# A hybrid decoder block on one core: the value projection of the recurrent layer in three float32r passes instead of native float32 products

## The chip, the cores and the metric

One core of a Trainium2 chip runs the whole program; the other cores are idle. The metric is the device time of one execution in microseconds (us), as the median of several runs. Before the change it is 1592.16 us (three runs, 1592.12 to 1593.12). Engines are named as the profile names them: PE is TensorE, DVE is VectorE, ACT is ScalarE, POOL is GpSimd, SP is SyncE, which issues the weight loads.

## What is computed

Two decoder layers over 272 tokens (16 meta tokens and 256 of the sequence), width 1024: sliding-window attention and a dense SwiGLU, then RWKV-7 time mixing and top-2-of-8 routed SwiGLU experts. The change sits in the time mixing of the second layer. Cut to what matters:

```python
xx = jnp.pad(h, ((0, 0), (1, 0), (0, 0)))[:, :-1] - h
xr, xw, xk, xv, xa, xg = [h + xx * mix[i] for i in range(N_MIX)]
r = xr @ w_r
k = xk @ w_k
v = xv @ w_v                       # 272 x 1024 by 1024 x 1024, float32
w = -jax.nn.softplus(-(w0 + jnp.tanh(xw @ w1) @ w2)) - 0.5
a = jax.nn.sigmoid(a0 + (xa @ a1) @ a2)
g = jax.nn.sigmoid(xg @ g1) @ g2
...
decay = jnp.exp(-jnp.exp(to_h(w)))
...                                # the recurrence over tokens, 16 heads of 64
return (y * g) @ w_o
```

## The kernel before

**Layout.** Activations of the recurrent layer lie with their 1024 channels as 8 chunks (KC) of 128 partitions, and the 272 tokens along the free dimension. A projection makes 8 output blocks of 128 channels (two heads each, a "pair"); a block is 8 matmuls of 128x128 weights against 128x272 activations, summed in one PSUM bank. `project(j)` does one block: j = 0 to 7 are keys, 8 to 15 receptance (r), 16 to 23 values. It takes PSUM bank j % 4, so it waits until ACT has copied out block j - 4 (`pr_ev`). The products are native float32: each matmul of the program shows as two records of the profile.

**The other form of product.** Elsewhere (attention, dense FFN, experts) the kernel forms float32 products from float32r passes. Operands are split into a high part (ACT: a copy to float32r, `ffn_high`) and a low part (DVE: the operand minus its high part, `ffn_low`); `split3` (lines 811 to 814) issues high x high, high x low and low x high.

**The order around the values.** Everything here is written out by hand, per engine, in program order; semaphores tie the engines.

- PE: key blocks; the small projections of decay, gates and step size (lines 1100 to 1127); then blocks 8 to 23 by `project`. After each of blocks 12 to 19 it does one `per_head` product (line 1087), which sums r times k over each head of a pair for the bonus term; it waits for that product's operand from DVE (`rk_ok`). After block 23 come the products of the recurrence (from line 1164 on).
- ACT, in its loop over j = 8 to 23: `take(j)` copies block j out of PSUM (line 1831); for j = 10 to 17 `decays(j - 10)`, three exponentials (lines 1866 to 1868), which wait for DVE's cumulative sums of that pair (`cum_ok`); for j = 13 to 20 it copies a bonus product out (line 1877).
- DVE: mixes the inputs (`mixes`, line 2352), among them the value input (`mixes(0, 3, ...)`), which goes to `xm[0]`; three long passes over keys and step sizes (lines 2394 to 2399); then a loop over the 8 pairs, in each of which: line 2405 makes the operand of `per_head` (`rk_ok`), line 2407 the scan, line 2410 the difference (`cum_ok`), then it waits for ACT's exponentials (`dec_exp`), and lines 2412 to 2416 scale five arrays.
- SP: weights of 2 MB in slots of SBUF. Slots 0 and 1 hold w_k, then w_r, then w_o; slots 2 and 3 hold the small matrices, then w_v. The two halves of w_o are loaded when blocks 8 to 11 and 12 to 15 are done (`pr_mm` 12 and 16). The queue then waits for the end of the recurrence (`ot_mm`, from line 1328 on PE) and starts the stream of the expert weights, which runs to the end of the program.

The lines that load the weights and that order the DVE loop:

```python
for s, w, n, s_, used in (..., (2, rwkv_w_v, 0, mix_used, 2),
                          (3, rwkv_w_v, 1, l2_mm, 24), (0, rwkv_w_o, 0, pr_mm, 12), (1, rwkv_w_o, 1, pr_mm, 16)):
    sp.wait_ge(s_, used)
    load(s, slot_k[s], cols(w[0], n))
```

Of the kernel before, what the change touches and what calls it, by code (L numbers as in the profile page):

```python
# [24 lines left out]
P = 128  # L25
# [45 lines left out]
def build(nc, x, meta_tokens, mixer_norm, ffn_norm, attn_w_qkv, attn_q_norm, attn_k_norm, attn_sinks, attn_w_o,  # L71
# [4 lines left out]
    with ctx:  # L76
        def sb(name, shape, dt=F32):
            return ctx.enter_context(nc.sbuf_tensor(name, shape, dt))
# [108 lines left out]
        with nc.sbuf_tensor("under_pT", [P, KC * T + 6 * HALF], F32), nc.sbuf_tensor("pT_hi", [P, 2, 8, P], F32R) as pT_hi, \  # L187
                nc.sbuf_tensor("pT_lo", [P, 2, 8, P], F32R) as pT_lo:
            pass
        arena = sb("arena", [P, ARENA])  # L190

        def area(off, *dims):
# [112 lines left out]
        ht_mm, ht_cp, yt_mm, yn_ok, gn_act, gn_ss, y_ok, wo2_mm, acc_ok = [sem(n) for n in (  # L305
            "ht_mm", "ht_cp", "yt_mm", "yn_ok", "gn_act", "gn_ss", "y_ok", "wo2_mm", "acc_ok")]
# [3 lines left out]
        sel_ok, xg_mm, xg_act, xg_dve, st_mm, st_ev, utok_hi_ok, utok_lo_ok, dn_mm, ye_hi_ok = [sem(n) for n in (  # L310
            "sel_ok", "xg_mm", "xg_act", "xg_dve", "st_mm", "st_ev", "utok_hi_ok", "utok_lo_ok", "dn_mm", "ye_hi_ok")]
# [3 lines left out]
        out_sem, utT_dve, own_mm = sem("out_sem"), sem("utT_dve"), sem("own_mm")  # L315
# [142 lines left out]
        def _(sp):  # L458
# [66 lines left out]
            for s, w, n, s_, used in ((0, rwkv_w_r, 0, pr_mm, 4), (1, rwkv_w_r, 1, pr_mm, 8), (2, rwkv_w_v, 0, mix_used, 2),  # L525
                                      (3, rwkv_w_v, 1, l2_mm, 24), (0, rwkv_w_o, 0, pr_mm, 12), (1, rwkv_w_o, 1, pr_mm, 16)):
                sp.wait_ge(s_, used)
                load(s, slot_k[s], cols(w[0], n))
# [214 lines left out]
        def _(pe):  # L743
# [309 lines left out]
            def project(j):  # L1053
                which, m = j // KC, j % KC
                cols_ = slice(META if which == 1 else 0, T)
                s = (0, 0, 2)[which] + m // 4
                if m == 0 and which:
                    pe.wait_ge(mix_ok, 3 + which)
                if m % 4 == 0:
                    pe.wait_ge(slot_in[s], 16 * {0: 1, 1: 1, 2: 4, 3: 5}[s] + (16 if which == 1 else 0))  # L1060
                if j >= 4:
                    pe.wait_ge(pr_ev, j - 3)
                for k in range(KC):
                    last = mm(ps[:, j % 4, cols_], slot_k[s][:, k, (m % 4) * P:(m % 4 + 1) * P], xm[(0, 1, 0)[which]][:, k, cols_],  # L1064
                              start=(k == 0), stop=(k == KC - 1))
                last.then_inc(pr_mm, 1)
# [323 lines left out]
            def tokens_turned(t, half):  # L1390
                pe.wait_ge(acc_ok, 2 * t + half + 1)
                if t == 0:
                    pe.wait_ge(yn_ok, 2)
                for q in range(4):
                    k = 4 * half + q
                    last = tr(ps[:, (6, 4)[t] + half, q * P:(q + 1) * P], acc[:, t, k * P:(k + 1) * P], ident[:, :])
                last.then_inc(utT_mm, 1)

            def logits(t, half):
                pe.wait_ge(*((utT_cp, 2 * t + half + 1) if 2 * t + half < 3 else (utT_dve, 1)))  # L1400
# [37 lines left out]
            with pe.Fori(0, n) as pas:  # L1438
# [25 lines left out]
                def turn(e):  # L1464
                    for t in range(2):
                        last = tr(ps[:, 5, t * P:(t + 1) * P], sel[:, t, e % 2, :].bitcast(F32), ident[:, :])
                    last.then_inc(st_mm, 1)
# [149 lines left out]
        def _(act):  # L1617
# [337 lines left out]
            def square_tokens(t):  # L1955
                act.wait_ge(acc_ok, 2 * t + 2)
# [147 lines left out]
        def _(dve):  # L2104
# [246 lines left out]
            def mix(k, buf, i, c0=0):  # L2351
                return v.scalar_tensor_tensor(xm[buf][:, k, c0:T], xx[:, k, c0:T], par[:, k, R_MIX + i:R_MIX + i + 1],
# [48 lines left out]

            dve.wait_ge(pads_zero, 3)
            for m in range(PAIRS):
# [6 lines left out]
                own.done(v.tensor_tensor(w_a[:, m, :], cum[:, m % 2, :], w_a[:, m, :], ALU.subtract), cum_ok)  # L2410
                dve.wait_ge(dec_exp, m + 1)
# [135 lines left out]
            def added(n):  # L2547
# [3 lines left out]
                own.done(v.tensor_tensor(acc[:, t, cs], htok[:, t, cs], ps[:, n, :], ALU.add), acc_ok)  # L2551
# [30 lines left out]
            own.done(v.tensor_copy(utT[:, 4:8, P:2 * P], ps[:, 5, :].rearrange("p (a b) -> p a b", a=4)), utT_dve)  # L2582
# [84 lines left out]
            with dve.Fori(0, n) as pas:  # L2667
# [15 lines left out]
                def gate_rows(e):  # L2683
                    dve.wait_ge(st_mm, pas + 1)
                    v.tensor_copy(selT[:, e % 2, :, :], ps[:, 5, 0:256].rearrange("p (a b) -> p a b", a=2)).then_inc(st_ev, 1)

                def collect(e, o, bank):
                    dve.wait_ge(es_mm, pas * 4 + (o + 1))
# [126 lines left out]
```

## Time and profile before

| | |
|---|---|
| runs | 1592.12, 1593.12, 1592.16 us (median 1592.16) |
| profiled execution | 1595.8 us, its span (first to last instruction) 1594.0 us |
| mean granted TensorE clock | 0.991 of full speed |
| PE busy | 1549.3 us, 97% of the span |
| DVE / ACT / POOL busy | 1219.7 / 1000.0 / 139.8 us |
| HBM read | 431.92 MB, 274 GB/s over the span |

The profiled execution is one execution of its own and 3.6 us above the median of the runs. Times in the trace count from the first instruction. In the trace the recurrent layer lies between about 397 and 655 us: the projections until 520 us, the recurrence until 609 us, then the output projection and the routing. The experts fill the rest. A matmul record lasts longer than the spacing between two records, since they are pipelined; a stretch of matmuls is therefore read from start to start.

### The profile page before, as it was taken

How to read it: one execution, taken by the hardware profiler on the slowest of the kernel's cores; microseconds unless marked ns; L12 is line 12 of the kernel's file. 1: busy time of each engine (PE TensorE's matmuls, PEld its weight loads, DVE VectorE, ACT ScalarE, POOL GpSimd, SP SyncE). 2: the span in 40 equal slices, each digit the busy share in tenths (PEclk: the TensorE clock that was granted, in tenths of full speed). 3: DMA queues.
4: the chain of work that ended last, by engine and by line, in shares of the span. 5: the costliest groups of instructions: out<-in, count | busy, mean ns of one | idle time of the engine just before them, and what ended most of it. 6: DMA issues, size and time to landing. Idle time of an engine off the chain costs nothing.

```text
span 1594.0 us, 26420 instructions
## 1 busy us (share of the span) xinstructions
PE 1549.3 (97%) x10509; PEld 1307.1 (82%) x10509; DVE 1219.7 (77%) x1165; ACT 1000.0 (63%) x1030; POOL 139.8 (9%) x195
## 2 busy tenths in 40 slices
PE   9999999999999989999999999999999999999998
PEld 7889999999778875788888888766788666788877
DVE  5565655633695574789888888999888989888898
ACT  5665344432243452577777777888777888767776
POOL 3464000000100640000000000000000000000200
PEclk9899999999999999899999999999999999999999
DMA  8105555544332006299999999999999999999996
GB/s 295 54 16 197 183 164 183 177 142 154 112 140 77 4 4 251 104 369 372 378 389 344 365 392 376 387 395 392 397 392 395 395 394 394 395 394 393 395 394 246
DMA packets 193199, 438.37 MB, mean 275 GB/s; under 512 B 10227, under 2 KB 11251, under 8 KB 193076
## 3 DMA queue, kind: packets, MB, share of 16 engines
q1 hardware_dynamic: 191452, 430.82, 73.5%
q0 software_dynamic: 1584, 5.77, 0.9%
q8 instruction: 85, 1.39, 0.4%
q14 instruction: 38, 0.31, 0.1%
q10 hardware_dynamic: 40, 0.08, 0.0%
HBM read 431.92 MB, written 4.72 MB: 274 GB/s over the span
## 4 chain that ended last, share of the span: by engine, by line
PE 79%; DVE 9%; DMA 5%; ACT 3%; issue 3%; DVEq 0%; ACTq 0%; SPq 0%; POOL 0%; POOLq 0%
PE ps L1503 13%; PE ps L1505 13%; PE ps L1504 13%; PE ps L812 7%; PE ps L814 6%; PE ps L813 6%; DVE wsplit L2673 5%; PE ps L1064 4%; DMA raw_w<-in_moe_w_up 3%; DMA raw_w<-in_moe_w_gate 3%; PE ps L1385 2%; ACT wsplit L1998 2%; PE ps L750 1%; PE ps L1541 1%; PE ps L1074 1%
## 5 line engine op out<-in xcount | busy, mean ns | idle before, releaser
L2673 DVE TENSOR_TENSOR wsplit<-raw_w,wsplit 128x2048 fp32r<-128x2048 f32 x336 | 754.4, 2286 | 68.6 <-ACT wsplit L1998 67.5
L1998 ACT ACTIVATE wsplit<-raw_w 128x2048 fp32r<-128x2048 f32 x336 | 629.9, 1920 | 78.7 <-DMA raw_w<-in_moe_w_up 31.2
L1503 PE MATMUL ps<-wsplit,xsplit 128*128 128x512 f32 x672 | 266.3, 396 | 3.4 <-DVE wsplit L2673 3.4
L1505 PE MATMUL ps<-wsplit,xsplit 128*128 128x512 f32 x672 | 262.1, 390 | 0.0
L1504 PE MATMUL ps<-wsplit,xsplit 128*128 128x512 f32 x672 | 261.7, 389 | 0.0
L1503 PEld LDWEIGHTS ps<-wsplit,xsplit 128*128 128x128 f32 x672 | 126.2, 188 | 30.8 <-DVE wsplit L2673 6.2
L1505 PEld LDWEIGHTS ps<-wsplit,xsplit 128*128 128x128 f32 x672 | 126.1, 188 | 27.2
L1504 PEld LDWEIGHTS ps<-wsplit,xsplit 128*128 128x128 f32 x672 | 126.4, 188 | 24.8
L2300 DVE TENSOR_TENSOR ffn_lo<-ffn_raw,ffn_hi 128x2048 fp32r<-128x2048 f32 x42 | 95.0, 2292 | 54.9 <-ACT ffn_hi L1787 54.7
L1503 PE MATMUL ps<-wsplit,hsplit 128*128 128x512 f32 x336 | 131.2, 390 | 2.2 <-DVE wsplit L2673 2.2
L1504 PE MATMUL ps<-wsplit,hsplit 128*128 128x512 f32 x336 | 130.8, 389 | 0.0
L1505 PE MATMUL ps<-wsplit,hsplit 128*128 128x512 f32 x336 | 130.8, 389 | 0.0
L814 PE MATMUL ps<-u_hi,ffn_lo 128*128 128x272 f32 x448 | 129.0, 288 | 0.0
L812 PE MATMUL ps<-u_hi,ffn_hi 128*128 128x272 f32 x448 | 128.9, 288 | 0.0
L813 PE MATMUL ps<-u_lo,ffn_hi 128*128 128x272 f32 x448 | 128.9, 288 | 0.0
L2048 ACT ACTIVATE arena<-ps 128x512 f32<-128x512 f32 x56 | 33.4, 596 | 110.5 <-PE ps L1505 110.5
L1530 PE MATMUL ps<-wsplit,xsplit 128*128 128x512 f32 x224 | 92.6, 414 | 10.3 <-DVE wsplit L2673 9.3
L1787 ACT ACTIVATE ffn_hi<-ffn_raw 128x2048 fp32r<-128x2048 f32 x42 | 78.6, 1904 | 37.8 <-PE ps L814 37.8
L1531 PE MATMUL ps<-wsplit,xsplit 128*128 128x512 f32 x224 | 87.8, 392 | 0.0
L812 PEld LDWEIGHTS ps<-u_hi,ffn_hi 128*128 128x128 f32 x448 | 84.6, 189 | 0.1
L813 PEld LDWEIGHTS ps<-u_lo,ffn_hi 128*128 128x128 f32 x448 | 84.2, 188 | 0.1
L814 PEld LDWEIGHTS ps<-u_hi,ffn_lo 128*128 128x128 f32 x448 | 84.1, 188 | 0.0
(476 smaller groups left out, 2547.7 us busy)
## 6 DMA issues: line engine op xcount, KB each, us to landing
raw_w<-in_moe_w_gate SPq DMA_DIRECT2D x114, 1024.0 KB, 10.6
raw_w<-in_moe_w_up SPq DMA_DIRECT2D x112, 1024.0 KB, 11.3
raw_w<-in_moe_w_down SPq DMA_DIRECT2D x112, 1024.0 KB, 10.5
ffn_raw<-in_ffn_w_up SPq DMA_DIRECT2D x14, 1024.0 KB, 5.2
ffn_raw<-in_ffn_w_gate SPq DMA_DIRECT2D x14, 1024.0 KB, 5.2
ffn_raw<-in_ffn_w_down SPq DMA_DIRECT2D x14, 1024.0 KB, 5.0
ffn_raw<-in_attn_w_qkv SPq DMA_DIRECT2D x6, 1024.0 KB, 10.7
ffn_raw<-in_attn_w_o SPq DMA_DIRECT2D x4, 1024.0 KB, 11.6
```

The lines of the kernel that those rows point to most:

```text
L812: mm(o, w_hi_, x_hi_, start=first, stop=False)
L813: mm(o, w_hi_, x_lo_, start=False, stop=False)
L814: return mm(o, w_lo_, x_hi_, start=False, stop=last_)
L1503: mm(o, x_[0], w_[0], start=first_, stop=False)
L1504: mm(o, x_[0], w_[1], start=False, stop=False)
L1505: return mm(o, x_[1], w_[0], start=False, stop=last_)
L1530: mm(o, both_parts(x_, k), whi[:, kk, :], start=(k == 0), stop=False)
L1531: last = mm(o, both_parts(x_, k), wlo[:, kk, :], start=False, stop=(k == KC - 1))
L1787: A(ffn_hi[:, m % NFH, :], ffn_raw[:, ffn_at(m), :], ACT.Copy).then_inc(hi_ok, 1)
L1998: A(wsplit[:, m % NRING, 0, :], raw_w[:, m % NRAW, :], ACT.Copy).then_inc(w_hi, 1)
L2300: v.tensor_tensor(ffn_lo[:, ffn_at(m), :], ffn_raw[:, ffn_at(m), :], ffn_hi[:, m % NFH, :].bitcast(F32), ALU.subtract).then_inc(lo_ok, 1)
L2673: v.tensor_tensor(wsplit[:, m % NRING, 1, :], raw_w[:, m % NRAW, :], wsplit[:, m % NRING, 0, :].bitcast(F32), ALU.subtract).then_inc(w_lo, 1)
```

## The change

The eight value blocks no longer use native float32 products. ACT makes the high part of the value input (one copy of 128x2176, `value_high(-1)`) and of the weights of each pair (eight copies of 128x1024), DVE the low parts (`value_low`), and PE calls `split3` 8 times per block. The low parts overwrite their sources in place; the high parts of the weights lie partly in slots 0 and 1, so w_o is loaded after block 23 (`pr_mm` 24). Three semaphores are merged to make room for two new ones (`v_part_hi`, `v_part_lo`). Cut to its core:

```diff
+        with nc.sbuf_tensor("under_vhi2", [P, KC * T], F32), nc.sbuf_tensor("vw_hi2", [P, 6, KC, P], F32R) as vw_hi2, \
...
+                nc.sbuf_tensor("xv_hi", [P, KC, T], F32R) as xv_hi:
+            pass
...
+        vw_raw = [raw_w[:, 2 * h:2 * h + 2, :].rearrange("p a (b n) -> p (a b) n", n=BLK) for h in range(2)]
+        vw_hi = [vw_hi0[:, m] for m in range(2)] + [vw_hi2[:, m] for m in range(6)]
...
-                                      (3, rwkv_w_v, 1, l2_mm, 24), (0, rwkv_w_o, 0, pr_mm, 12), (1, rwkv_w_o, 1, pr_mm, 16)):
+                                      (3, rwkv_w_v, 1, l2_mm, 24), (0, rwkv_w_o, 0, pr_mm, 24), (1, rwkv_w_o, 1, pr_mm, 24)):
...
                 if j >= 4:
                     pe.wait_ge(pr_ev, j - 3)
-                for k in range(KC):
+                if which == 2:
+                    pe.wait_ge(v_part_hi, m + 2)
+                    pe.wait_ge(v_part_lo, m + 2)
+                for k in range(KC) if which == 2 else ():
+                    last = split3(ps[:, j % 4, 0:T], vw_hi[m][:, k, :], vw_lo[:, m // 4, k, (m % 4) * P:(m % 4 + 1) * P],
+                                  xv_hi[:, k, :], xv_lo[:, k, :], k == 0, k == KC - 1)
+                for k in range(KC) if which < 2 else ():
...
+            def value_high(m):
+                if m < 0:
+                    act.wait_ge(mix_ok, 5)
+                    A(xv_hi[:, :, :], xv_raw[:, :, :], ACT.Copy).then_inc(v_part_hi, 1)
+                    return
+                act.wait_ge(slot_in[2 + m // 4], 16 * (4 + m // 4))
+                if m >= 2:
+                    act.wait_ge(pr_mm, KC + (4 if m < 6 else 8))
+                A(vw_hi[m], vw_raw[m // 4][:, :, (m % 4) * P:(m % 4 + 1) * P], ACT.Copy).then_inc(v_part_hi, 1)
+
             act.wait_ge(kk_done, 1)
             for j in range(KC, 3 * KC):
                 take(j)
+                if j == KC:
+                    value_high(-1)
+                elif j == KC + 1:
+                    value_high(0)
+                    value_high(1)
+                elif KC + 3 <= j <= 2 * KC:
+                    value_high(j - KC - 1)
                 if 10 <= j < 18:
                     decays(j - 10)
...
+            def value_low(m):
+                dve.wait_ge(v_part_hi, m + 2)
+                if m < 0:
+                    v.tensor_tensor(xv_lo[:, :, :], xv_raw[:, :, :], xv_hi[:, :, :].bitcast(F32), ALU.subtract).then_inc(v_part_lo, 1)
+                    return
+                cs = slice((m % 4) * P, (m % 4 + 1) * P)
+                v.tensor_tensor(vw_lo[:, m // 4, :, cs], vw_raw[m // 4][:, :, cs], vw_hi[m].bitcast(F32),
+                                ALU.subtract).then_inc(v_part_lo, 1)
+
+            value_low(-1)
             dve.wait_ge(pads_zero, 3)
             for m in range(PAIRS):
                 dve.wait_ge(pr_ev, KC + 1 + m)
...
                 own.done(v.tensor_tensor(w_a[:, m, :], cum[:, m % 2, :], w_a[:, m, :], ALU.subtract), cum_ok)
+                value_low(m)
                 dve.wait_ge(dec_exp, m + 1)
```

How the instructions stand on three engines. On DVE, from the last long pass over all keys to the second pair of the loop; the line numbers of the changed kernel are 10 to 43 higher. Before:

```order
L2399 TENSOR_TENSOR arena<-arena 128x8x272
L2405 SCALAR_TENSOR_TENSOR arena<-arena,par 128x256
L2407 SCALAR_TENSOR_TENSOR arena<-reset,arena 128x320
L2410 TENSOR_TENSOR arena<-arena 128x320
L2412 TENSOR_TENSOR arena<-arena 128x256
L2413 COPY chunkdecay<-arena 128x5
L2414 TENSOR_TENSOR arena<-arena 128x320
L2415 TENSOR_TENSOR arena<-arena 128x320
L2416 SCALAR_TENSOR_TENSOR arena<-arena 128x320
L2405 SCALAR_TENSOR_TENSOR arena<-arena,par 128x256
```

and now:

```order
L2432 TENSOR_TENSOR arena<-arena 128x8x272
L2438 TENSOR_TENSOR xv_lo<-xv_raw,xv_hi 128x2176
L2448 SCALAR_TENSOR_TENSOR arena<-arena,par 128x256
L2450 SCALAR_TENSOR_TENSOR arena<-reset,arena 128x320
L2453 TENSOR_TENSOR arena<-arena 128x320
L2441 TENSOR_TENSOR vw_lo<-raw_w,vw_hi0 128x8x128
L2456 TENSOR_TENSOR arena<-arena 128x256
L2457 COPY chunkdecay<-arena 128x5
L2458 TENSOR_TENSOR arena<-arena 128x320
L2459 TENSOR_TENSOR arena<-arena 128x320
L2460 SCALAR_TENSOR_TENSOR arena<-arena 128x320
L2448 SCALAR_TENSOR_TENSOR arena<-arena,par 128x256
```

The low part of the value input (L2438) stands ahead of the whole loop, and the low part of one pair's weights (L2441) in each of its eight rounds, between the difference and the first of the scaled arrays.

On ACT, from the last copies of the gate blocks to the second set of exponentials, before:

```order
L1859 ACTIVATE arena<-ps 128x256 x2
L1831 ACTIVATE arena<-ps 128x256 x3
L1866 ACT_TABLE_LOAD
L1866 ACTIVATE arena<-arena 128x320
L1867 ACTIVATE arena<-arena 128x320
L1868 ACTIVATE arena<-arena 128x320
L1831 ACTIVATE arena<-ps 128x256
L1866 ACTIVATE arena<-arena 128x320
```

and now:

```order
L1875 ACTIVATE arena<-ps 128x256 x2
L1847 ACTIVATE arena<-ps 128x256
L1889 ACTIVATE xv_hi<-xv_raw 128x2176
L1847 ACTIVATE arena<-ps 128x256
L1894 ACTIVATE vw_hi<-raw_w 128x1024 x2
L1847 ACTIVATE arena<-ps 128x256
L1882 ACT_TABLE_LOAD
L1882 ACTIVATE arena<-arena 128x320
L1883 ACTIVATE arena<-arena 128x320
L1884 ACTIVATE arena<-arena 128x320
L1847 ACTIVATE arena<-ps 128x256
L1894 ACTIVATE vw_hi<-raw_w 128x1024
```

The high parts stand behind the copies out of PSUM, six of them one per round ahead of the exponentials.

On SP the order is the same and the waits differ only in their counts:

```order
L473 DMA raw_w<-in_rwkv_w_v 128x8x512 [waits mix_used]
L473 DMA raw_w<-in_rwkv_w_v 128x8x512 [waits l2_mm]
L473 DMA arena<-in_rwkv_w_o 128x8x512 [waits pr_mm] x2
L565 DMA arena<-in_ffn_norm 128x1024 [waits ot_mm]
L562 DMA raw_w<-in_moe_w_gate 128x4x512 [waits w_lo] x2
```

Nothing stands between the two loads of w_o and the wait for the end of the recurrence, so a later load of w_o holds back no other load that is due before that wait ends.

## Rows read from the trace of the kernel before

**Rows 1.** The page: busy time of PE; the chain that ended last, by line

```profile
PE 1549.3 (97%) x10509; PEld 1307.1 (82%) x10509; DVE 1219.7 (77%) x1165; ACT 1000.0 (63%) x1030; POOL 139.8 (9%) x195
...
PE ps L1503 13%; PE ps L1505 13%; PE ps L1504 13%; PE ps L812 7%; PE ps L814 6%; PE ps L813 6%; DVE wsplit L2673 5%; PE ps L1064 4%; DMA raw_w<-in_moe_w_up 3%; DMA raw_w<-in_moe_w_gate 3%; PE ps L1385 2%; ACT wsplit L1998 2%; PE ps L750 1%; PE ps L1541 1%; PE ps L1074 1%
```

**Rows 2.** Stretches (blocks 16-19, 20-23, recurrence): PE PEld DVE ACT POOL, clock, DMA

```profile
488.79:505.18 16.39, 16.39 (x73) 13.68 (x72) 11.29 (x27) 6.38 (x19) 0.00 (x0) 1.00 0.36 129
505.18:520.00 14.82, 14.82 (x65) 11.97 (x63) 4.41 (x12) 2.88 (x10) 0.00 (x0) 1.00 0.00 0
520.00:549.00 29.00, 28.47 (x933) 25.92 (x934) 15.15 (x25) 13.14 (x23) 16.66 (x16) 1.00 0.02 5
```

**Rows 3.** Timeline of PE: start us, us, line, shape, count [idle before]

```profile
488.79 3.83 PE L1064 MATMUL ps<-arena 128*128 128x272 f32 x16
492.46 0.59 PE L1087 MATMUL ps<-arena,headones 128*128 128x256 f32 x2
...
504.75 0.59 PE L1087 MATMUL ps<-arena,headones 128*128 128x256 f32 x2
505.18 14.83 PE L1064 MATMUL ps<-arena 128*128 128x272 f32 x64
520.55 1.16 PE L1166 MATMUL ps<-arena 64*64 64x64 f32 x64 [0.53 <-issue]
```

**Rows 4.** Float32r matmuls of line 812: ns min/median/max, first and last start

```profile
L812 PE MATMUL ps<-u_hi,ffn_hi x448: 284/287/492, 139.2 to 308.6; 128*128 128x272 f32 x150
```

**Rows 5.** Timeline of DVE, the last long passes and the loop over pairs

```profile
467.50 2.42 DVE L2399 TENSOR_TENSOR arena<-arena 128x2176 f32<-128x2176 f32 x1
469.95 0.48 DVE L2405 SCALAR_TENSOR_TENSOR arena<-arena,par 128x256 f32<-128x256 f32 x1
...
471.20 0.49 DVE L2410 TENSOR_TENSOR arena<-arena 128x320 f32<-128x320 f32 x1
472.95 0.43 DVE L2412 TENSOR_TENSOR arena<-arena 128x256 f32<-128x256 f32 x1 [1.25 <-ACT arena L1868]
...
474.57 0.48 DVE L2405 SCALAR_TENSOR_TENSOR arena<-arena,par 128x256 f32<-128x256 f32 x1
...
502.24 0.48 DVE L2405 SCALAR_TENSOR_TENSOR arena<-arena,par 128x256 f32<-128x256 f32 x1
```

**Rows 6.** Timeline of ACT: blocks 8 and 9 taken, last exponential of pairs 0 and 7

```profile
463.15 0.38 ACT L1831 ACTIVATE arena<-ps 128x256 f32<-128x256 f32 x1 [3.13 <-PE ps L1064]
466.55 0.38 ACT L1831 ACTIVATE arena<-ps 128x256 f32<-128x256 f32 x1 [3.01 <-PE ps L1064]
...
472.46 0.45 ACT L1868 ACTIVATE arena<-arena 128x320 f32<-128x320 f32 x1
...
504.75 0.45 ACT L1868 ACTIVATE arena<-arena 128x320 f32<-128x320 f32 x1
```

**Rows 7.** Groups by form, 280 to 300 us: splits of 128x1088 in the FFN

```profile
L2335 DVE TENSOR_TENSOR hid_lo<-hid,hid_hi 128x1088 fp32r<-128x1088 f32 x1 | 1.3, 1293 | 1.2 <-ACT hid_hi L1812 1.2
...
L1812 ACT ACTIVATE hid_hi<-hid 128x1088 fp32r<-128x1088 f32 x1 | 1.1, 1112 | 8.0 <-DVE hid L2333 8.0
```

**Rows 8.** Timeline of SP: issue of w_v, of w_o, and the end of its wait

```profile
446.44 13.55 SPq L463 DMA_DIRECT2D arena<-in_rwkv_w_v  x2
473.44 15.48 SPq L463 DMA_DIRECT2D arena<-in_rwkv_w_o  x2
...
609.49 0.35 SPq L555 DMA_DIRECT2D arena<-in_ffn_norm  x1
```

**Rows 9.** The page's DMA issues: KB each, median us from issue to landing

```profile
arena<-in_rwkv_w_o SPq DMA_DIRECT2D x2, 2048.0 KB, 8.2
```

**Rows 10.** Timeline of PE: the first matmuls that read w_o

```profile
609.38 7.13 PE L1385 MATMUL ps<-arena 128*128 128x512 f32 x16
```

**Rows 11.** The chain that ended last, a piece among the experts

```profile
1100.24 13.71 DMA raw_w<-in_moe_w_gate
```

**Rows 12.** Groups by form, 655 to 1590 us: the experts' low parts

```profile
L2673 DVE TENSOR_TENSOR wsplit<-raw_w,wsplit 128x2048 fp32r<-128x2048 f32 x335 | 752.1, 2286 | 68.6 <-ACT wsplit L1998 67.5
```

More of the change, by code:

```diff
@@ L189, in build @@
             pass
+        with nc.sbuf_tensor("under_vhi2", [P, KC * T], F32), nc.sbuf_tensor("vw_hi2", [P, 6, KC, P], F32R) as vw_hi2, \
+                nc.sbuf_tensor("under_vlo", [P, 2 * KC * P], F32), nc.sbuf_tensor("vw_lo", [P, 2, KC, BLK], F32R) as vw_lo, \
+                nc.sbuf_tensor("vw_hi0", [P, 2, KC, P], F32R) as vw_hi0, nc.sbuf_tensor("under_xv", [P, KC * T - 2 * KC * P], F32), \
+                nc.sbuf_tensor("xv_lo", [P, KC, T], F32R) as xv_lo, nc.sbuf_tensor("under_xvhi", [P, 2 * KC * BLK - 2 * KC * T], F32), \
+                nc.sbuf_tensor("xv_hi", [P, KC, T], F32R) as xv_hi:
+            pass
+        with nc.sbuf_tensor("under_xvraw", [P, 2 * KC * T + 4 * KC * BLK], F32), nc.sbuf_tensor("xv_raw", [P, KC, T], F32) as xv_raw:
+            pass
+        vw_raw = [raw_w[:, 2 * h:2 * h + 2, :].rearrange("p a (b n) -> p (a b) n", n=BLK) for h in range(2)]
+        vw_hi = [vw_hi0[:, m] for m in range(2)] + [vw_hi2[:, m] for m in range(6)]
         arena = sb("arena", [P, ARENA])
@@ L304, in build @@
             "rhs_mm", "rhs_ev", "u_mm", "u_ev", "ot_mm", "gb_ok", "s_mm", "s_ok", "rank_next")]
[L305 to L306 removed]
+        ht_mm, ht_cp, yt_mm, yn_ok, gn_act, gn_ss, y_ok, wo2_mm, acc_utT_ok = [sem(n) for n in (
+            "ht_mm", "ht_cp", "yt_mm", "yn_ok", "gn_act", "gn_ss", "y_ok", "wo2_mm", "acc_utT_ok")]
         n4_std_exp, utok_ok, utT_mm, utT_cp, choice_mm, choice_ok = [sem(n) for n in (
@@ L525, in _ @@
             for s, w, n, s_, used in ((0, rwkv_w_r, 0, pr_mm, 4), (1, rwkv_w_r, 1, pr_mm, 8), (2, rwkv_w_v, 0, mix_used, 2),
-                                      (3, rwkv_w_v, 1, l2_mm, 24), (0, rwkv_w_o, 0, pr_mm, 12), (1, rwkv_w_o, 1, pr_mm, 16)):
+                                      (3, rwkv_w_v, 1, l2_mm, 24), (0, rwkv_w_o, 0, pr_mm, 24), (1, rwkv_w_o, 1, pr_mm, 24)):
                 sp.wait_ge(s_, used)
-                load(s, slot_k[s], cols(w[0], n))
+                load(s, vw_raw[n] if w is rwkv_w_v else slot_k[s], cols(w[0], n))
             we_g = moe_w_gate[0].rearrange("e (k p) n -> e p k n", p=P)
@@ L1390, in tokens_turned @@
             def tokens_turned(t, half):
-                pe.wait_ge(acc_ok, 2 * t + half + 1)
+                pe.wait_ge(acc_utT_ok, 2 * t + half + 1)
                 if t == 0:
@@ L1399, in logits @@
             def logits(t, half):
-                pe.wait_ge(*((utT_cp, 2 * t + half + 1) if 2 * t + half < 3 else (utT_dve, 1)))
+                pe.wait_ge(*((utT_cp, 2 * t + half + 1) if 2 * t + half < 3 else (acc_utT_ok, 5)))
                 for k in range(4 * half, 4 * half + 4):
@@ L1466, in turn @@
                         last = tr(ps[:, 5, t * P:(t + 1) * P], sel[:, t, e % 2, :].bitcast(F32), ident[:, :])
-                    last.then_inc(st_mm, 1)
+                    last.then_inc(es_mm, 1)
                 def scatter(e, o, bank):
@@ L2351, in mix @@
             def mix(k, buf, i, c0=0):
-                return v.scalar_tensor_tensor(xm[buf][:, k, c0:T], xx[:, k, c0:T], par[:, k, R_MIX + i:R_MIX + i + 1],
+                return v.scalar_tensor_tensor((xm[buf] if i != 3 else xv_raw)[:, k, c0:T], xx[:, k, c0:T], par[:, k, R_MIX + i:R_MIX + i + 1],
                                               uT[:, k, 1 + c0:T + 1], ALU.mult, ALU.add)
@@ L2550, in added @@
                 cs = slice(h * BLK, (h + 1) * BLK)
-                own.done(v.tensor_tensor(acc[:, t, cs], htok[:, t, cs], ps[:, n, :], ALU.add), acc_ok)
+                own.done(v.tensor_tensor(acc[:, t, cs], htok[:, t, cs], ps[:, n, :], ALU.add), acc_utT_ok)
             def root(t):
@@ L2581, in _ @@
             dve.wait_ge(utT_mm, 4)
-            own.done(v.tensor_copy(utT[:, 4:8, P:2 * P], ps[:, 5, :].rearrange("p (a b) -> p a b", a=4)), utT_dve)
+            own.done(v.tensor_copy(utT[:, 4:8, P:2 * P], ps[:, 5, :].rearrange("p (a b) -> p a b", a=4)), acc_utT_ok)
             root(1)
```

12 lines of the change are left out of this document (6 added, 6 removed).

## Prediction

> **What bounds the kernel now.** I read the page first. PE is busy for 97% of the span, and nearly all of the chain that ended last is PE's or the experts' splits; line 1064, the native projections, has 4% of it [rows 1]. So a microsecond taken off those projections can be worth a microsecond, if PE really is what waits for nothing there. The stretches say so for both halves of the value blocks: PE is busy without a gap from 488.79 to 520.00 us, at a granted clock of 1.00, which is the 2.4 GHz level [rows 2]. The PE timeline gives the unit: block 16 starts at 488.79 and the per-head product behind it at 492.46, so a block takes 3.67 us. From a per-head product to the next block it is 0.43 us (504.75 to 505.18). Blocks 20 to 23 run back to back from 505.18 for 14.83 us, to 520.01, and the recurrence starts at 520.55 [rows 3].
>
> The second thing to read is DVE. Its loop over pairs starts at 469.95; the next round starts at 474.57 and the eighth at 502.24, so seven rounds take 32.29 us, 4.61 each [rows 5]. Each round begins with the operand (0.48 us) of the per-head product that PE does behind block 12 + m. The eighth operand is ready at 502.24 + 0.48 = 502.72, and PE wants it at 504.75 [rows 3, 5]: 2.03 us of slack today. That slack is what the change runs into.
>
> **PE alone.** Removed: 64 native products, 8 blocks of 3.67 us. Added: 192 float32r matmuls of 128x272. The dense FFN has the same shape and the same `split3`: in its first part 1344 such matmuls (448 on each of three lines) start between 139.2 and 308.6 us, that is 169.4 / 1343 = 0.126 us each [rows 4]. So a block becomes 24 x 0.126 = 3.03 us and saves 0.64 us; all eight save 5.1 us. That is the most PE can get by this row. A native block spread over four passes per product is 3.67 / 32 = 0.115 us per pass, so the two rows price a pass differently; I take the FFN's, because it is the very instruction, shape and clock.
>
> The Trainium skill counts in passes ("FP8 and Floating Point Precision", TensorE Precision Notes: true FP32 takes four passes through the array). By that rule three passes would be 3/4 of 3.67, or 2.75 us a block. The FFN's spacing disagrees with it by a tenth.
>
> **DVE ahead of the loop.** New is the low part of the value input, 128x2176. It stands behind the pass of line 2399, which is of the same size and takes 2.42 us, and the following instruction started 2.45 us after it (467.50 to 469.95), with a settling wait in it. I take 2.35 us for the shift of the whole loop; 2.2 to 2.5 would do. Its high part is ready in time: ACT is free between blocks 8 and 9, 463.53 to 466.55 [rows 6], and a copy of 128x2176 is twice the 128x1088 copy of 1.11 us [rows 7], so it ends near 465.8, before 469.95.
>
> **DVE in the loop.** New in each round is a low part of 128x1024. Between the row of 128x1088 (1.293 us) [rows 7] and those of 128x320 (0.49) [rows 5] it comes to 1.23 us. In a round the difference ends at 471.69 (1.74 us in), and DVE then idles 1.25 us until ACT's third exponential ends at 472.91 [rows 5, 6]. The low part goes exactly there: 471.69 + 1.23 = 472.92. I cost it at nothing; its cover is this wait, and if the cover fails the price is up to 1.23 us a round. It needs its high part: those of pairs 0 and 1 follow block 9 on ACT (466.9, some 1.05 us each by the 1.11 of rows 7, so done by 469.1, before block 10 and before the exponentials), the others are made one round ahead of the pair. w_v's second half is issued near 460.0 and lands about 8.2 us later [rows 8, 9], well before its first reader behind block 13. ACT's work in a round grows by 1.05 us to about 3 us of 4.61. Nothing.
>
> **PE with DVE's gate.** The operands now come at 469.95 + 2.35 + 4.61 m + 0.48: 491.2 (m = 4), 495.8, 500.4 and 505.1 (m = 7). PE needs them behind blocks 16 to 19. Block 16 starts at 488.79 as before (the r blocks before it are not touched, and their gates keep a slack of over 1 us), ends at 491.8, no wait. Block 17 starts at 492.25, ends at 495.3 and waits 0.5. Block 18 then runs from 496.4 to 499.4 and waits 1.0; block 19 from 501.0 to 504.0 and waits 1.1. With 0.1 us for the signal and 0.43 behind the per-head product, block 20 starts at 505.60 instead of 505.18: **0.42 us later**, in spite of four faster blocks. Blocks 20 to 23 have no per-head product behind them; their low parts are ready (the last, pair 7's, at about 507.6) and they gain 4 x 0.64 = 2.56 us. PE reaches the recurrence 2.56 - 0.42 = **2.1 us** earlier. What else the recurrence needs: the DVE loop ends near 509.3 instead of 506.9, still ahead of 517.9.
>
> **SP.** w_o's two loads go from 473 and 489 us to about 518. At 8.2 us each [rows 9] they land by 535; they are first read at 609.38 [rows 10]. Nothing. They now run under the recurrence, where DMA was idle (share 0.02) and PE issues most densely, 933 matmuls in 29 us [rows 2]. No row shows that stretch with a transfer in it, so: between 0 and, if instruction supply suffered, the 0.5 us of one "issue" gap [rows 3] a few times. I take 0. The merged semaphores cost nothing: waits stay where they were.
>
> **Does it survive the experts?** The expert stream is issued when the recurrence ends on PE (609.49) [rows 8], so transfers, PE and splits all move by the same 2.1 us. Sum against the profiled execution: 1595.8 - 2.1 = 1593.7. That execution is 3.6 us above the median of the runs; against the median, 1592.16 - 2.14 = **1590.0 us**.
>
> **The rivals.**
> *The gate does not hold* (say, the operands keep their slack because DVE catches up): PE gains the whole 5.1 us, 1587.0. Against it: a DVE round has no idle time left but what the low part takes. 5%.
> *A float32r pass costs what a native pass costs*, 0.115 us: a block saves 0.92, and 4 x 0.92 - 0.42 = 3.3 us, 1588.9. For it: the native block's own rate. Against it: 1344 matmuls at 0.126 us. The Trainium skill's pass count, cited above, is this case. 7%.
> *The experts swallow it*: they have their own balance of transfers and splits, such as a wait of 13.7 us for a gate tile [rows 11], and if some fixed point there decides, the time stays at 1592.2. Against it: the stream has no start of its own. 12%.
> *DVE's loop becomes the bound, and the kernel gets slower.* Place: the low part in each round. If it does not fit into the 1.25 us, because it starts only when its high part comes or because the strided read takes longer, each round grows by d and block 20 by 7 d. Fully exposed, d = 1.23: block 20 starts 8.6 us later, the sum is 2.1 - 8.6, and the time 1598.7. It turns slower from d = 0.31. For it: the fit is exact on paper, with nothing to spare. Against it: a contiguous split of twice the size runs at 2.286 us in the experts [rows 12], no sign of a slow form, and the start of an instruction overlaps the end of the one before. 8%, counting the milder cases that still end 3 us up.
> The forecast has the remaining 68%. Its own range is a gain of 1 to 3.2 us: d between -0.05 and 0.1, the shift 2.2 to 2.5, waits of PE on two more semaphores per block at up to 0.1.
>
> **The numbers.** 1590.0 us. A measurement of this kernel can tell about 0.2%, 3.2 us, from no change. Faster by more than that are the gate that does not hold (5%), most of the pass-cost case (6%, since 3.3 is just over) and the forecast's upper tail (8%): 19%. Slower by more is the DVE case, 8%. The rest, 73%, is within 0.2%, though most of it on the faster side. The range of 8 in 10 runs from 1588.0, which takes in the pass-cost case, to 1593.0, which takes in the swallowed gain and a little scatter.
>
> **What would show it.** Right: blocks of the value projection at 3.03 us from start to start; PE idle before the per-head products behind blocks 17 to 19, released by line 2448 on DVE; DVE rounds of 4.61 us from 472.3 on with hardly any idle time; block 20 at about 505.6; the recurrence at about 518.4 instead of 520.55; the first expert load at about 607.4; and from there the same length to the end. Wrong: blocks at 2.75 us; no idle time on PE before line 1103; DVE rounds over 4.9 us; a recurrence that is longer than its 89 us while w_o lands; or an expert stage that is longer by what was won.

## The result, and the profile after

The changed kernel is slower, by a little: 1595.76 us (median of 20 runs, 1593.22 to 1598.1) against 1593.25 us for the kernel before in 20 runs (1591.33 to 1596.17); the ratio is 1.0015, with a 95% interval of 1.0009 to 1.0021. By the ratio that is 2.4 us more, and the forecast was 2.1 us less. The median of the kernel before rose by 1.1 us with the further runs (1592.16 in the first three), but even with the range moved up by that, to 1594.1 us, the time lies outside it, and on the other side of no change.

The two profiled executions must not be compared by their spans. The one of the changed kernel is 2.5 us shorter (1591.5 against 1594.0). But they part long before the change. At 64.9 us, when the attention stage begins, they are within 0.1 us of each other; at its output projection, 107 us before and 102.6 us after, they are 4.3 us apart. In between, the granted clock of the one before was 0.50, the 1.2 GHz level, from about 68 to 82 us, and that of the one after was not. Two rows, busy time from 70 to 100 us, before and after; the clock, a mean over the stretch, is the third column from the right:

```profile
70.00:100.00 30.00, 29.97 (x189) 24.47 (x190) 22.83 (x86) 20.08 (x70) 12.56 (x16) 0.80 0.08 28
```

```profile
70.00:100.00 30.00, 28.66 (x217) 23.53 (x218) 26.09 (x97) 22.87 (x80) 15.44 (x20) 1.00 0.08 30
```

So I count from the start of block 8, the first block of the loop that the change touches: at 459.44 us before, at 455.08 us after. First the PE timeline of the kernel before at that place, then of the changed kernel:

```profile
459.44 17.43 PE L1064 MATMUL ps<-arena 128*128 128x256 f32 x80
```

```profile
455.08 17.43 PE L1080 MATMUL ps<-arena 128*128 128x256 f32 x80
...
491.56 0.70 PE L1103 MATMUL ps<-arena,headones 128*128 128x256 f32 x2 [0.49 <-DVE arena L2448]
...
496.17 0.70 PE L1103 MATMUL ps<-arena,headones 128*128 128x256 f32 x2 [0.90 <-DVE arena L2448]
...
500.79 0.70 PE L1103 MATMUL ps<-arena,headones 128*128 128x256 f32 x2 [0.90 <-DVE arena L2448]
...
514.12 1.16 PE L1182 MATMUL ps<-arena 64*64 64x64 f32 x64 [0.53 <-issue]
...
517.89 0.44 PE L1180 MATMUL ps<-arena 64*64 64x128 f32 x7
519.96 1.85 PE L1180 MATMUL ps<-arena 64*64 64x128 f32 x57 [1.62 <-issue]
...
524.41 0.44 PE L1192 MATMUL ps<-arena 64*64 64x64 f32 x6
526.18 0.86 PE L1192 MATMUL ps<-arena 64*64 64x64 f32 x23 [1.33 <-issue]
...
607.77 7.13 PE L1401 MATMUL ps<-arena 128*128 128x512 f32 x16
```

These rows answer to [rows 3] and [rows 10]. Three stretches come out of them:

| us | before | after | difference |
|---|---|---|---|
| block 8 to the recurrence | 61.11 | 59.04 | -2.07 |
| recurrence, to the first matmul that reads w_o | 88.83 | 93.65 | +4.82 |
| from there to the end | 984.62 | 983.73 | -0.89 |

The first line is the forecast's gain. The second takes more than twice that away. Its two rows of 1.62 and 1.33 us with "issue" are PE sitting still between two matmuls of one line. In [rows 3] the first matmul of the recurrence has an "issue" row too, with 0.53 us, and so it has here; the two others are new at that place.

The recurrence falls into two parts. The first, from its first matmul to the first of line 1239 (1255 in the changed kernel), is the one in which w_o now lands; I call it the dense part. Before, then after:

```profile
547.53 4.77 PE L1239 MATMUL ps<-arena 64*64 64x64 f32 x158
```

```profile
544.94 4.78 PE L1255 MATMUL ps<-arena 64*64 64x64 f32 x158
```

It takes 26.98 us before and 30.82 after: 3.84 of the 4.82 us. The remaining 0.98 us lies in the rest, 61.85 us before and 62.83 after, where no w_o is in flight any more. There the kernel before has small "issue" rows of its own, with no load beside them:

```profile
590.91 0.33 PE L1319 MATMUL ps<-arena 64*64 64x64 f32 x4 [0.24 <-issue]
...
595.38 0.27 PE L1328 MATMUL ps<-arena 64*64 64x64 f32 x2 [0.77 <-issue]
```

The changed kernel has 0.70 and 0.54 us in the same place.

The third line of the table is scatter: over the ten profiles of this study, all with the same code from there on, it lies between 982.9 and 985.2 us.

What runs at that moment is the load of w_o. The timeline of SP, which answers to [rows 8], and time to landing, which answers to [rows 9]:

```profile
513.62 0.99 SPq L473 DMA_DIRECT2D arena<-in_rwkv_w_o  x2
...
607.88 0.35 SPq L565 DMA_DIRECT2D arena<-in_ffn_norm  x1
```

```profile
arena<-in_rwkv_w_o SPq DMA_DIRECT2D x2, 2048.0 KB, 11.4
```

Both halves are issued half a microsecond before the recurrence starts, and they fill the DMA engines until about 527 us.

The splits are where they were planned. DVE in the changed kernel, answering to [rows 5]: the start of the loop, one round, and the start of the last round.

```profile
465.60 2.42 DVE L2438 TENSOR_TENSOR xv_lo<-xv_raw,xv_hi 128x2176 fp32r<-128x2176 f32 x1
467.94 0.48 DVE L2448 SCALAR_TENSOR_TENSOR arena<-arena,par 128x256 f32<-128x256 f32 x1
...
469.19 0.49 DVE L2453 TENSOR_TENSOR arena<-arena 128x320 f32<-128x320 f32 x1
469.59 1.22 DVE L2441 TENSOR_TENSOR vw_lo<-raw_w,vw_hi 128x1024 fp32r<-128x1024 f32 x1
470.93 0.43 DVE L2456 TENSOR_TENSOR arena<-arena 128x256 f32<-128x256 f32 x1
...
500.26 0.48 DVE L2448 SCALAR_TENSOR_TENSOR arena<-arena,par 128x256 f32<-128x256 f32 x1
```

The low part of a pair's weights takes 1.22 us and fills the hole from 469.59 to 470.93; a round stays (500.26 - 467.94) / 7 = 4.62 us. Counted from block 8, the loop starts at 12.86 instead of 10.51 us: 2.35 us later, to the hundredth.

### The profile page after: what moved, and what is told of

It reads as the page before. It is cut to its first block, busy times and chain, and to the rows that moved or that the text cites. A ratio compares the mean times of both kernels' runs of the same rounds, so it can differ in the third digit from the quotient of the medians.

```text
span 1591.5 us, 26581 instructions
## 1 busy us (share of the span) xinstructions
PE 1537.3 (97%) x10573; PEld 1300.3 (82%) x10573; DVE 1231.1 (77%) x1174; ACT 1009.8 (63%) x1039; POOL 139.1 (9%) x195
## 4 chain that ended last, share of the span: by engine, by line
PE 74%; DVE 12%; DMA 5%; issue 4%; ACT 4%; DVEq 0%; ACTq 0%; POOL 0%; SPq 0%; POOLq 0%
PE ps L1519 13%; PE ps L1521 13%; PE ps L1520 13%; PE ps L822 7%; PE ps L824 7%; PE ps L823 7%; DVE wsplit L2717 5%; DMA raw_w<-in_moe_w_up 4%; DMA raw_w<-in_moe_w_gate 2%; PE ps L1401 2%; ACT wsplit L2031 2%; PE ps L1557 1%; PE ps L1090 1%; PE ps L1080 1%; DVE arena L2420 1%
```

## The experiments

Two theories stood at the start. **A**: the 4 MB of w_o, moved under the recurrence, hold up PE's supply of instructions there. **B**: the PE program is longer (its profile has 64 more matmuls, and as many weight loads; the 187 instructions of the expectations stand in no run), and that alone moves where it stalls. A third, **G**, is the forecast's own: DVE's shifted loop gates PE through the per-head products. In this section the two times are "block 8 to the recurrence" and "recurrence", from each run's one profile; they were 61.11 and 88.83 us before, 59.04 and 93.65 in the changed kernel. The dense part of the recurrence is given beside them (26.98 us before, 30.82 in the changed kernel). Ratios are to the kernel before, measured again beside the experiments: 1593.45 us for the late w_o in full, the paced one, the early one in two loads and the low part on POOL, 1592.66 us for the other four.

### w_o late, and nothing else

```diff
-(0, rwkv_w_o, 0, pr_mm, 12), (1, rwkv_w_o, 1, pr_mm, 16)
+(0, rwkv_w_o, 0, pr_mm, 24), (1, rwkv_w_o, 1, pr_mm, 24)
```

(in the kernel before)

> The kernel before with only the counts of the two w_o loads changed (pr_mm 24 instead of 12 and 16); native products, no split, PE's program is the same. Theory A (the 4 MB of w_o, now running while PE issues most densely, hold up PE's supply of instructions): gaps named 'issue' of some 3 us in the first 15 us of the recurrence, the recurrence (first matmul of line 1166 to first of line 1385) 92.5 to 93.8 us instead of 88.8, total 3 to 5 us above before. Theory B (the longer PE program, 187 instructions more, shifts where its blocks of instructions are fetched; w_o is incidental): recurrence 88.8 us, total within 1 us of before.

Measured: 61.12 and 94.14 us, total 1598.8 us, ratio 1.0035 (1.0022 to 1.0048). PE's program is instruction for instruction that of before, and the recurrence is 5.3 us longer, somewhat more than theory A had said. All of it is in the dense part (32.29 us); the rest takes 61.85 us as before. The PE timeline has one long gap, inside line 1164:

```profile
519.58 1.16 PE L1166 MATMUL ps<-arena 64*64 64x64 f32 x64 [0.53 <-issue]
...
529.78 0.60 PE L1164 MATMUL ps<-arena 64*64 64x128 f32 x8
533.25 3.26 PE L1164 MATMUL ps<-arena 64*64 64x128 f32 x54 [2.87 <-issue]
```

B is out as the cause of the loss: the late load alone makes it. That the load acts through PE's supply of instructions is not shown by this run, but by the packets below. The gap accounts for 2.9 of the 5.3 us. Another 1.6 us or so is the clock. Behind the gap the granted clock was 0.50, the 1.2 GHz level, for 3.4 us:

```profile
533.50:533.70 0.20, 0.20 (x8) 0.20 (x8) 0.00 (x0) 0.00 (x0) 0.00 (x0) 0.50 0.00 0
```

and the 54 products of line 1164 behind the gap took 3.19 us to the start of the next line, where 64 of them take 1.91 us at a granted clock of 1.00 in the kernel before. Without that, the price of this run would be 3.7 us, close to that of the changed kernel (3.84 us, all of it at 1.00).

### Half of it late

```diff
-(0, rwkv_w_o, 0, pr_mm, 12), (1, rwkv_w_o, 1, pr_mm, 16)
+(0, rwkv_w_o, 0, pr_mm, 12), (1, rwkv_w_o, 1, pr_mm, 24)
```

(in the kernel before)

> The kernel before with only the second half of w_o (2 MB) loaded after block 23, the first half where it was. Theory A as a matter of how long transfers and dense issue overlap: about half the price of the whole, recurrence 91 to 92 us (88.83 before, 94.14 with both halves late). If instead any queue of 2 MB costs one missed block of instructions and no more: 91.7 us or so as well, but one gap of about 2.9 us; if the price begins only with the second transfer: under 89.5 us.

Measured: 61.11 and 89.99 us, total 1594.57 us, ratio 1.001 (1.0 to 1.0019). The dense part takes 27.68 us: half the bytes cost 0.70 us there, where the whole cost 5.3, or 3.7 without the clock. The price is far from proportional. The PE timeline has one new gap there, of 0.37 us. The other 0.46 us of the recurrence lie in the rest (62.31 us), behind the load. None of the three expectations had this size.

### The same bytes in the same stretch, but paced

```diff
-(3, rwkv_w_v, 1, l2_mm, 24), (0, rwkv_w_o, 0, pr_mm, 24), (1, rwkv_w_o, 1, pr_mm, 24)):
+(3, rwkv_w_v, 1, l2_mm, 24)):
...
+            for i, (s_, used) in enumerate([(pr_mm, 24)] + [(grp_mm, n) for n in (4, 8, 11, 15, 18, 22, 25)]):
+                sp.wait_ge(s_, used)
+                load(i // 4, slot_k[i // 4][:, 2 * (i % 4):2 * (i % 4) + 2, :], cols(rwkv_w_o[0], i // 4)[:, 2 * (i % 4):2 * (i % 4) + 2, :])
```

(in the changed kernel; `grp_mm` counts the groups of products of the recurrence, and PE's waits for w_o count the pieces)

> The changed kernel with w_o in eight loads of 512 KB, each issued some four product groups after the last (one about every 4 us), so the same bytes pass in the same recurrence but never 4 MB queued at once. Theory A in its form 'instruction fetches queue behind megabytes of transfers': the two gaps of 1.6 and 1.3 us shrink to under 0.5 us in sum, recurrence 89 to 90.5 us, total about 2 to 4 us below the changed kernel, at or up to 2 us below before. If any transfer at all beside dense issue costs the same per byte: gaps sum to about 3 us again, spread over eight places, recurrence 93 us. Theory B: two gaps at the same places as in the changed kernel, 93.7 us.

Measured: 59.04 and 90.59 us, total 1592.35 us, ratio 0.9998 (0.9989 to 1.0006). Three of the 4.8 us are back although all 4 MB still pass under the recurrence, nearly all under its dense part (28.33 us). The DMA view of this run, 513 to 548 us, shows how they pass (tenths busy in 40 slices, then GB/s):

```profile
DMA  0079109910049539502871880485667000000000
GB/s 0 0 183 386 49 0 185 379 54 0 0 91 344 183 59 330 211 19 51 264 283 28 229 325 14 98 339 201 77 234 288 19 0 0 0 9 19 0 0 0
```

Between the pieces the engines fall idle, and the PE timeline has one gap of 0.53 us there where the changed kernel had 1.62 and 1.33. Breaking the transfer takes away 2.5 of the 3.8 us of the dense part. It does not take away all: the same 4 MB in pieces still cost 1.35 us, more than 2 MB in one piece. So how long the transfer runs without a pause counts for most, but the bytes are not free.

### w_o early

The high parts of pairs 6 and 7 go to where the mixed input of the r blocks (`xm[1]`) lay, so slot 1 is free after block 15; slot 0 is free after block 21.

```diff
-nc.sbuf_tensor("vw_hi2", [P, 6, KC, P], F32R) as vw_hi2, \
+nc.sbuf_tensor("vw_hi2", [P, 4, KC, P], F32R) as vw_hi2, \
...
+        with nc.sbuf_tensor("under_vhi6", [P, 4 * KC * BLK + 3 * KC * T], F32), nc.sbuf_tensor("vw_hi6", [P, 2, KC, P], F32R) as vw_hi6:
+            pass
...
-(0, rwkv_w_o, 0, pr_mm, 24), (1, rwkv_w_o, 1, pr_mm, 24)):
+(1, rwkv_w_o, 1, pr_mm, 16), (0, rwkv_w_o, 0, pr_mm, 22)):
```

> The changed kernel with the high parts of pairs 6 and 7 in the place of the mixed input that the r blocks have used up, so the second half of w_o is loaded after block 15 and the first after block 21 (about 6 us before the recurrence). Only some 2 us of one load still overlap the recurrence. Theory A: recurrence 88.8 to 90.0 us, the recurrence still starts 2.1 us earlier than before (59.0 us after block 8's start against 61.1), total 1 to 2 us below before. Theory B: recurrence 93.7 us, total as the changed kernel, about 2.4 us above before.

Measured: 59.03 and 89.37 us, total 1591.49 us, ratio 0.9989 (0.998 to 0.9997). The dense part takes 26.98 us, to the hundredth what it took before. The loss is gone but for 0.5 us, and the gain of the front is kept. Is the 0.5 us the last overlap? The next run loads the first half in four pieces, each as the place of one high part comes free:

```diff
+            for i in range(4):
+                sp.wait_ge(pr_mm, 19 + i)
+                load(0, slot_k[0][:, 2 * i:2 * i + 2, :], cols(rwkv_w_o[0], 0)[:, 2 * i:2 * i + 2, :])
```

> The changed kernel with w_o early as in e6 (second half after block 15, first half in four pieces after blocks 18 to 21) and the per-head products where the change has them. Against e3 (recurrence 89.37 us) this takes the last overlap away. Theory A: recurrence 88.8 to 89.1 us, start still 59.0 us after block 8, total 2 to 2.5 us below before. If the 0.5 us that e3 kept comes from the longer PE program and not from the overlap: 89.4 us again.

Measured: 59.03 and 89.58 us, total 1590.68 us, ratio 0.999 (0.9981 to 0.9999). With the transfers done before the recurrence starts, it still takes 0.75 us more than before. So that part is not the overlap, and the dense part says the same: 26.98 us again. The 0.5 to 0.7 us of both runs lie in the rest of the recurrence, where the small "issue" rows are. Over the ten profiles the rest takes 61.85, 61.85 and 62.31 us with the PE program of before and 62.17 to 62.99 us with the longer one. That may be theory B in a small form. But the first group varies by 0.46 us with one and the same program, and there is one profile of each kernel, so it stays open.

### The gate: the low part of the value input on POOL

```diff
+            pool.wait_ge(v_part_hi, 1)
+            one(g.tensor_tensor(xv_lo[:, :, :], xv_raw[:, :, :], xv_hi[:, :, :].bitcast(F32), ALU.subtract), pads_zero)
...
-            value_low(-1)
```

(in the changed kernel, whose PE then waits for `pads_zero` 4 ahead of block 16)

> The changed kernel with the low part of the value input (128x2176) made by POOL, which idles there, instead of by DVE; w_o as in the changed kernel. If my gate is right (DVE's loop, shifted 2.35 us by that pass, sets blocks 17 to 20): the DVE loop starts 2.4 us earlier, PE has no idle time before the per-head products up to block 18, block 20 starts about 1.9 us earlier against block 8 than in the changed kernel, and the recurrence starts about 57.1 us after block 8 (59.0 in the changed kernel, 61.1 before). The recurrence itself is unchanged at 93.7 us under theory A. Total about 1.9 us below the changed kernel. If the gate is elsewhere (ACT's copies or PE's own rate): recurrence at 59.0 us, no gain. A pass of POOL of this size may take 5 to 6 us and slow DVE beside it; if it holds DVE up by as much as it saves, nothing is won either, and the DVE rows show it.

Measured: 61.31 and 95.48 us, total 1598.37 us, ratio 1.0034 (1.0021 to 1.0046). It is slower than the changed kernel, and two groups of this run, 463 to 471 us, say why:

```profile
L2437 DVE TENSOR_TENSOR arena<-arena 128x2176 f32<-128x2176 f32 x1 | 7.0, 7033 | 0.0
L704 POOL TENSOR_TENSOR xv_lo<-xv_raw,xv_hi 128x2176 fp32r<-128x2176 f32 x1 | 6.7, 6650 | 51.4 <-ACT xv_hi L1894 51.4
L2436 DVE TENSOR_TENSOR arena<-arena 128x2176 f32<-128x2176 f32 x1 | 2.4, 2426 | 0.0
```

Lines 2436 and 2437 are twins: each multiplies two inputs of the same size. The first began before POOL's pass and took 2.4 us; the second began during it and took 7.0, as if it had stood still until POOL was done. The loop started 2.3 us later than in the changed kernel, not 2.4 earlier, and so did the recurrence (61.31 against 59.04). That confirms the gate from the wrong side: what shifts DVE's loop shifts PE by the same amount. The Trainium skill has the rule ("SBUF — State Buffer", SBUF: two separate sides): POOL and a DVE instruction with two SBUF inputs take turns on a shared pair of ports, for the whole instruction. The times agree with it, in both directions. The DVE pass of 7.03 us started at 463.63 us and ended at 470.66, 2.3 us after POOL's, which ended at 468.38. And POOL's own pass, from 461.73 us on, had started during the pass of line 2436, which ended at 463.72; if it stood still until then, POOL itself needed some 4.7 of its 6.65 us (an estimate from these rows). The recurrence is 1.8 us longer than in the changed kernel although w_o is loaded in the same way; part of that is the clock, which was granted at 0.50 (1.2 GHz) for 3.4 us of its dense part (32.49 us), as in the first experiment.

### The gate from the right side: per-head products one block later

```diff
-                if 12 <= j < 20:
-                    if j == 12:
+                if 13 <= j < 21:
+                    if j == 13:
                         pe.wait_ge(l2_ev, 24)
-                    per_head(j - 12, v_a, rk_ok, rk_mm, rk_ev)
+                    per_head(j - 13, v_a, rk_ok, rk_mm, rk_ev)
```

> The changed kernel with each per-head product one block later on PE (behind blocks 13 to 20 instead of 12 to 19); w_o as in the changed kernel. Theory G (DVE's shifted loop gates PE through these products, and through nothing else): PE has no idle time in blocks 16 to 23, the recurrence starts 55.9 us after block 8 (59.04 in the changed kernel: 0.49 + 0.90 + 0.90 us of visible waits and some 0.9 around them go), DVE rounds stay 4.61 us. The recurrence stays 93 to 94.5 us by theory A, and the total comes 3 us below the changed kernel, at before or just under it. Rival: the waits move to the low parts of the weights or to ACT's copies, and the recurrence starts at 57.5 to 59 us.

Measured: 56.01 and 93.66 us, total 1592.96 us, ratio 0.9998 (0.9989 to 1.0007). The waits of PE in the value blocks are gone, and the recurrence starts 3.0 us earlier against block 8. G holds. The recurrence is as long as in the changed kernel, 93.66 and 93.65 us, but that the two agree so well is chance: the gaps here are 2.28 and 1.35 us and the dense part takes 31.49 us, 0.67 more than there, and the rest 0.66 less.

### Both together

The per-head products one block later, and w_o early in pieces as above.

> The per-head products one block later, and w_o early: its second half after block 15, its first half in four pieces of 512 KB after blocks 18 to 21, as each high part's place comes free (the high parts of pairs 6 and 7 lie where the mixed input of r was). Theories A and G together: recurrence starts 55.9 us after block 8 and takes 88.8 to 89.4 us; the total is 4.5 to 5.5 us below before (ratio 0.9965 to 0.9972), faster beyond noise, and faster than any other variant. If A and G both hold but the gains do not add (the earlier recurrence runs into the last piece): recurrence 90 us or more.

Measured: 55.99 and 89.37 us, total 1588.13 us, ratio 0.997 (0.9958 to 0.9982). It is faster than both kernels, and the parts add: 5.1 us won in front, 0.5 us lost in the recurrence (its dense part takes 26.98 us), 4.6 in sum; the medians differ by 4.5. Its first matmul of the recurrence and its first that reads w_o:

```profile
511.88 1.16 PE L1187 MATMUL ps<-arena 64*64 64x64 f32 x64 [0.53 <-issue]
```

```profile
601.25 7.13 PE L1406 MATMUL ps<-arena 128*128 128x512 f32 x16
```

## Why the prediction was wrong

**PE alone: right.** A block was to take 3.03 us. In the changed kernel ACT takes blocks 20 on at that distance:

```profile
507.58 0.40 ACT L1847 ACTIVATE arena<-ps 128x272 f32<-128x272 f32 x1 [2.35 <-PE ps L824]
510.60 0.40 ACT L1847 ACTIVATE arena<-ps 128x272 f32<-128x272 f32 x1 [2.63 <-PE ps L824]
```

The rival with 2.75 us a block, three quarters of a native block, is out, and with it the Trainium skill's pass count, cited in the prediction, as a measure of time. The four blocks 20 to 23 with the step to the recurrence take 12.98 us, 15.37 before: 2.39 us won, forecast as 2.56.

**DVE ahead of the loop and in it: right.** Shift 2.35 us, low part 1.22 us for 1.23, round 4.62 us for 4.61. The rival that DVE's loop becomes the bound did not occur: its d was 0.01.

**The gate: right.** The three waits were forecast at 0.5, 1.0 and 1.1 us and were 0.49, 0.90 and 0.90. Block 20 starts 0.32 us later against block 8 (46.06 us behind it, 45.74 before), forecast as 0.42. The gain up to the recurrence was forecast at 2.1 us and was 2.07 (2.39 less 0.32): each term is right to 0.2 us, and that the sum is right to a few hundredths is luck. Undoing the gate gave 3.0 us more, and worsening it took 2.3 away.

**SP: wrong, and this is the step that failed.** The text put w_o's new place right, saw that DMA was idle there and that PE "issues most densely", bounded the cost between 0 and "the 0.5 us of one 'issue' gap a few times", and took 0. In the changed kernel the recurrence grew by 4.8 us. 3.8 of them are in the dense part, under the load, and they are gone, to the hundredth, in all three runs that load w_o ahead of the recurrence; in the old kernel with w_o late the dense part grew by 5.3 us. The other 1.0 us of the changed kernel lies in the rest of the recurrence, and w_o is not shown to cause it. The fault was to price the step by the slack of the load (it lands some 80 us before its first reader) and to leave its effect on a bystander at the lower end of the bound. The list of signs did name "a recurrence that is longer than its 89 us while w_o lands", but no rival had it and so no chance. An open upper end should have widened the range on the slow side, and been named as the likeliest way to be slower.

The bound rested on the wrong row as well. The 0.53 us ahead of the first matmul of the recurrence stand in all ten profiles alike, and the last packet of q8 (see below) ended about 15 us or more before them, so they say nothing of the supply. The rows that do were in the trace of before, later in the recurrence: 0.24 and 0.77 us at 590.91 and 595.38 us, where PE ran dry with no load beside it.

**The experts: right.** The stage moved with the recurrence: its first load (`in_ffn_norm`) is issued 0.11 us behind the first matmul that reads w_o, as before, and its length is within scatter.

**The balance.** -2.07, +4.82 and -0.89 us of scatter make +1.86 us in the pair of profiles; the runs say +2.4 (0.15%, at least 0.09%). The prediction gave 73% to a time within 0.2% of no change, and the time is there, but by luck: a gain that was right and a loss that was left out cancel in part.

**What holds PE up.** For the gaps in the dense part the profile only says that PE waits for nothing that it knows of ("issue"). The packets of the DMA view say what it waits for. They name the packets that carry instructions, for the changed kernel (516 to 528 us) and for the kernel before (516 to 535 us):

```profile
q1 hardware_dynamic: 1962, 3.95, 87.3%
q8 instruction: 3, 0.05, 1.7%
```

```profile
q8 instruction: 3, 0.05, 1.2%
q14 instruction: 1, 0.01, 0.2%
```

Three packets of some 16 KB took 1.7% of 16 engines' time in 12 us, that is 1.1 us each, and without w_o 1.2% of 19 us, 1.2 us each. The packet itself is not slower. It starts late. I follow q8, whose packets turn out to keep time with PE's gaps. The start of a single packet is found by narrowing the window of the view until one is left in it. In the changed kernel, whose recurrence starts at 514.12 us, the window 514.12 to 517.45 us has none, and 517.45 to 517.55 us has the first:

```profile
q1 hardware_dynamic: 400, 0.82, 81.6%
```

```profile
q1 hardware_dynamic: 19, 0.04, 100.8%
q8 instruction: 1, 0.02, 65.1%
```

(The share is that of so short a window and says nothing.) In the changed kernel with w_o early, whose recurrence starts at 514.95 us, it is there from 515.90 to 515.95 us:

```profile
q8 instruction: 1, 0.02, 146.9%
```

The starts of the first two packets of q8, in us after the first matmul of the recurrence, each run with w_o in the dense part below the one with the same PE program without it:

| | first | second | late by |
|---|---|---|---|
| kernel before | 1.73 | 6.00 | |
| w_o late, nothing else | 4.33 | 11.29 | 2.60, 5.29 |
| half of it late | 4.60 | 8.05 | 2.87, 2.05 |
| changed, w_o early | 0.98 | 4.49 | |
| changed | 3.38 | 9.63 | 2.40, 5.14 |
| changed, w_o in eight pieces | 2.44 | 6.05 | 1.46, 1.56 |
| both together | 1.07 | 4.53 | |
| per-head products one block later | 4.09 | 10.27 | 3.02, 5.74 |

The delays go with the prices, though not in proportion. Under the unbroken 4 MB the second packet is over 5 us late (in part because the first was late and PE stood still between them), and the dense part costs 3.8 to 5.3 us more. Under half of w_o, which is through at 7.9 us, the second packet is 2 us late, under the eight pieces 1.6 us, and the dense part costs 0.7 and 1.35 us more. And the gaps keep time with the packets: in the ten profiles the recurrence has 31 "issue" gaps besides the one ahead of its first matmul, of 0.17 to 2.87 us, and every one of them ends 1.20 to 1.48 us after a packet of q8 has ended. In the changed kernel the two packets end at 4.41 and 10.76 us, and PE goes on at 5.84 and 12.06. So PE waits for its instructions, in the dense part under w_o and, for shorter times, later on in every kernel. What makes a packet start late beside an unbroken transfer, no row shows; it stays open.

The Trainium skill ("Runtime: NRT & Kernel Launch", Instruction fetch mechanics) says that instructions are streamed in blocks of 16 KiB over a DMA queue of the engine's own, and that the cost of crossing into the next one is mostly hidden. The packets of some 16 KB agree with the first. The cost was hidden in the dense part of the kernel before, not quite in the rest of its recurrence (0.24 and 0.77 us), and not under 4 MB in one piece.

## What to carry to other kernels

A load that is moved has two prices: whether it is in time, and what it does to the engines that run beside it. Where PE issued small instructions at its densest, 933 matmuls in 29 us, even an idle DMA system was not free to use, since PE's own instructions come over it. Keep transfers out of such a stretch, or make them short and let pauses fall between the pieces. Small "issue" gaps in the profile of before are the warning, but look which of them follow a packet of instructions. And when a chain of short steps is cut on one engine, look for the product that ties it to a second engine's loop; the faster arithmetic was worth 5.1 us here, and 3.0 of them came only when that product moved by one step in the order.

## What the runs showed that I had not expected

- 4 MB of weights in one stretch beside the dense part cost 3.8, 4.5, 5.3 and 5.5 us in four kernels (the last two with 3.4 us at the 1.2 GHz level in it); 2 MB cost 0.7; 4 MB in eight pieces with pauses 1.35; and nothing when they landed before it.
- Each of 31 gaps of PE without a visible wait ended 1.20 to 1.48 us after a 16 KB packet of instructions.
- A POOL pass of 128x2176 took 6.65 us, some 2.0 of them under a DVE pass that had started before it, and stretched the next DVE pass of the same size from 2.43 to 7.03 us.
- The 128x272 float32r matmul keeps a distance of 0.126 us, where a quarter of the native product takes 0.115.
- Two profiled executions can differ by 4.4 us before the first changed instruction, nearly all of it by the granted clock of one stage (a mean of 0.80 or 1.00 over 30 us). Stretches measured from a common instruction agree to a few hundredths: 61.11, 61.12 and 61.11 us in three kernels with the same front, and 26.98 us for the dense part in four kernels with no load beside it.
